# Wide first-layer products for the mixer's spatial tiles and the second gated step, with the halves added on VectorE

## The reference, cut to what matters

```python
def even_mixer(h, w_in, conv_w, pool_w, pool_scale, w_out):
    z = h @ w_in                                  # 256 x 1024 @ 1024 x 2048
    gate_b = z[..., :A_W]                         # A_W = 512
    gate_c = z[..., A_W:2 * A_W]
    val = z[..., 2 * A_W:3 * A_W]
    pool_in = z[..., 3 * A_W:]
    y_a = gate_b * causal_dwconv(gate_c * val, conv_w)
    y_b = multiscale_pool(pool_in, pool_w, pool_scale)
    return jnp.concatenate([y_a, y_b], axis=-1) @ w_out

def conv_ffn(h, w_in, conv_w, conv_b, w_out):     # D_FF = 2816
    z = h @ w_in
    u, g = z[..., :D_FF], z[..., D_FF:]
    a = causal_dwconv(u, conv_w) + conv_b
    return (jax.nn.silu(a) * g) @ w_out
```

## Time and profile before

| | |
|---|---|
| time, median of 3 runs (lowest to highest) | 1242.0 us (1241.77 to 1242.34) |
| span of the profiled execution, first to last instruction | 1240.0 us |
| TensorE matmuls, busy | 1226.5 us, 99% of the span |
| VectorE busy | 967.7 us, 78% |
| ScalarE busy | 703.3 us, 57% |
| GpSimd busy | 135.4 us, 11% |
| DMA | 214 GB/s mean |
| chain that ended last | TensorE 87%, VectorE 8%, ScalarE 2% |

### The profile page before, as it was taken

How to read it: one execution, slowest core, us unless ns; L and a number is a source line. 1 busy time by engine, 2 the same in 40 slices (tenths; PEclk the granted TensorE clock), 3 DMA queues, 4 the chain that set the end, 5 groups by cost and what they waited for, 6 DMA issues and landing times.

```text
span 1240.0 us, 18559 instructions
## 1 busy us (share of the span) xinstructions
PE 1226.5 (99%) x7013; PEld 1063.4 (86%) x7013; DVE 967.7 (78%) x1218; ACT 703.3 (57%) x1061; POOL 135.4 (11%) x249
## 2 busy tenths in 40 slices
PE   8999999999999999999999999999999999999998
PEld 7989888888778989998889888888888998888887
DVE  5867999977885798898788688997685898676654
ACT  6555555556465555555677566555564243755552
POOL 5000000010000211111133201120010010000000
PEclk9999999999999999999999999999999999999999
DMA  9746777665562798893132448997456587386540
GB/s 325 236 153 219 241 248 239 223 198 182 184 204 68 236 331 309 314 334 115 55 122 69 137 170 291 392 391 262 170 200 208 171 309 267 123 292 211 179 160 34
DMA packets 153649, 265.77 MB, mean 214 GB/s; under 512 B 6092, under 2 KB 110480, under 8 KB 153584
## 3 DMA queue, kind: packets, MB, share of 16 engines
q1 hardware_dynamic: 134560, 204.75, 48.8%
q0 software_dynamic: 18544, 59.65, 13.7%
q10 hardware_dynamic: 480, 0.49, 0.1%
HBM read 263.78 MB, written 1.08 MB: 214 GB/s over the span
## 4 chain that ended last, share of the span: by engine, by line
PE 87%; DVE 8%; ACT 2%; issue 2%; POOL 1%; DMA 0%; POOLq 0%; ACTq 0%; DVEq 0%
PE ps L1948 24%; PE ps L1928 17%; PE ps L1931 9%; PE ps L1914 4%; PE ps L1913 4%; PE ps L1912 4%; DVE w_lo L1141 2%; PE ps L1991 2%; PE ps L1992 2%; PE ps L1993 2%; PE ps L2055 2%; PE ps L1969 2%; PE ps L1971 2%; PE ps L1970 2%; PE ps L2057 2%
## 5 line engine op out<-in xcount | busy, mean ns | idle before, releaser
L1141 DVE TENSOR_TENSOR w_lo<-raw,w_hi 128x2048 fp32r<-128x2048 f32 (+3 forms) x211 | 434.1, 2071 | 32.2 <-ACT w_hi L580 31.9
L580 ACT ACTIVATE w_hi<-raw 128x2048 fp32r<-128x2048 f32 (+3 forms) x213 | 368.7, 1737 | 61.6 <-PE ps L1948 51.1
L1928 PE MATMUL ps<-xn,w_hi 128*128 128x512 f32 x976 | 244.9, 393 | 0.1
L1928 PEld LDWEIGHTS ps<-xn,w_hi 128*128 128x128 f32 x976 | 178.3, 189 | 35.3 <-issue 1.6
L1931 PEld LDWEIGHTS ps<-xn,w_lo 128*128 128x128 f32 x976 | 133.1, 190 | 9.6
L1931 PE MATMUL ps<-xn,w_lo 128*128 128x256 f32 x976 | 136.1, 283 | 0.0
L1948 PE MATMUL ps<-w_hi,a_hi 128*128 128x512 f32 x432 | 134.7, 393 | 0.2 <-DVE a_lo L1853 0.2
L661 ACT ACTIVATE work<-ps 128x512 f32<-128x512 f32 x61 | 36.3, 594 | 171.7 <-PE ps L1931 171.7
L1948 PE MATMUL ps<-w_lo,a_hi 128*128 128x512 f32 x432 | 133.6, 390 | 0.0
L1948 PE MATMUL ps<-w_hi,a_lo 128*128 128x512 f32 x432 | 133.3, 390 | 0.0
L1912 PE MATMUL ps<-xn,w_hi 128*128 128x256 f32 x432 | 122.8, 284 | 0.0
(11 more groups left out here) (362 smaller groups left out, 2007.7 us busy)
## 6 DMA issues: line engine op xcount, KB each, us to landing
raw<-in_ffn_w SPq DMA_DIRECT2D x64, 1024.0 KB, 5.6
side<-in_ada_w POOLq DMA_DIRECT2D x96, 512.0 KB, 6.1
raw<-in_ffn_w_in SPq DMA_DIRECT2D x40, 1024.0 KB, 5.2
raw<-in_ffn_w_out SPq DMA_DIRECT2D x32, 512.0 KB, 5.2
raw<-in_gm_w_in SPq DMA_DIRECT2D x16, 1024.0 KB, 6.5
raw<-in_od_w_in SPq DMA_DIRECT2D x12, 1024.0 KB, 5.4
raw<-in_gm_w_out SPq DMA_DIRECT2D x8, 1024.0 KB, 5.7
raw<-in_ev_w_in SPq DMA_DIRECT2D x7, 1024.0 KB, 12.4
```

The costliest lines, as they stand in the source:

```text
L580: nc.scalar.activation(w_hi[s][:, 0:w], raw[s][:, 0:w], ACT.Copy).then_inc(hi_done, 1)
L1141: nc.vector.tensor_tensor(w_lo[s][:, 0:w], raw[s][:, 0:w], w_hi[s][:, 0:w].bitcast(F32), ALU.subtract)\
L1928: nc.tensor.matmul(o, hi, xn[:, 512 * k:512 * k + 512], start=k == 0, stop=False)
```

## The change

1. The six tiles of the first mixer become `f_wide`, into banks 0/1, 4/5, 6/7, 0/1, 2/3, 0/1. ScalarE's copy of gate_c is removed. A new helper `halves_added` adds the two halves of a bank pair in one VectorE instruction, a `tensor_reduce` over a strided view of PSUM: for each output it reads the element at column t and the one at column t + 256. It stands for gate_c (into SBUF), for val and for gate_b (each into `ev_in` in SBUF, followed by the multiplication, which waits for it).
2. TensorE's waits for free banks change with the banks: tile 5 now waits for `EV["gate"]` 1 and tile 7 for `EV["gate"]` 2.
3. Step 1 of the gated layers: the u tile is `f_wide` in both layers, the g tile in the first; `low_copy` and `join` are now also run for step 1, the transposed head goes to banks 4 and 5, and one TensorE wait for `prod` before the loop goes.

The core of the diff:

```diff
-            ev_c = wk(6144, 512)
             ev_cv = wk(2048, 2 * 258).rearrange("p (b t) -> p b t", b=2)
...
             for m in range(2):
                 t = T_EV + 2 + 3 * m
-                act.wait_ge(w_used, t + 1)
-                nc.scalar.activation(ev_c, ps[3 * m % 4][:, :], ACT.Copy).then_inc(EV["gate"], 1)
                 split(t + 4)
...
-                    src = ps[0 if j.c else 2]
-                    if j.c >= 2:
+                    src = ps[4]
+                    if j.c:
                         low_copy(f_u, 0)
...
-                    if j.c >= 2 and n == 0:
+                    if j.c and n == 0:
                         act.wait_ge(w_used, val(u + 2))
                         low_copy(f_g, 2)
...
+            def halves_added(x, bank):
+                v = banks[:, 512 * bank:512 * bank + 1024].rearrange("p (b c t) -> p b t c", b=2, c=2)
+                return nc.vector.tensor_reduce(pair(x), v, AX.X, ALU.add)
...
             for m in range(2):
                 t = T_EV + 2 + 3 * m
+                dve.wait_ge(w_used, t + 1)
+                halves_added(wk(6144, 512), 0).then_inc(EV["gate"], 1)
+                dve.wait_ge(w_used, t + 2)
+                chain(halves_added(ev_in, (4, 2)[m]))
                 dve.wait_ge(EV["gate"], m + 1)
-                dve.wait_ge(w_used, t + 2)
-                nc.vector.tensor_tensor(ev_cv[:, :, 2:258], ps[(1 + 3 * m) % 4][:, :].rearrange("p (b t) -> p b t", b=2),
-                                        ev_c, ALU.mult).then_inc(EV["prod"], 1)
+                nc.vector.tensor_tensor(ev_cv[:, :, 2:258], pair(ev_in), ev_c, ALU.mult).then_inc(EV["prod"], 1)
...
                 dve.wait_ge(w_used, t + 3)
-                nc.vector.tensor_tensor(ev_y, ps[(2 + 3 * m) % 4][:, :], ev_a, ALU.mult).then_inc(EV["y"], 1)
+                chain(halves_added(ev_in, (6, 0)[m]))
+                nc.vector.tensor_tensor(ev_y, ev_in, ev_a, ALU.mult).then_inc(EV["y"], 1)
...
-                    x = ps[0 if j.c else 2]
-                    if j.c >= 2:
+                    x = ps[4]
+                    if j.c:
                         join(f_u, 0, u_join(j))
                         x = f_u
...
-                    x = ps[3 if j.c == 0 else 1 if j.c == 1 else 2]
-                    if j.c >= 2 and n == 0:
+                    x = ps[2 if j.c else 5]
+                    if j.c and n == 0:
                         join(f_g, 2, u_join(j) + 1)
...
-            free = {4: (EV["pool"], 1), 5: (EV["pool"], 2), 6: (EV["gate"], 1), 7: (EV["prod"], 1)}
+            free = {2: (head_cp, 2 * HEAD["ev"] + 1), 5: (EV["gate"], 1), 6: (EV["pool"], 2), 7: (EV["gate"], 2)}
             head("ev", T_EV)
-            for m in range(2, 8):
+            for m, bank in zip(range(2, 8), (0, 4, 6, 0, 2, 0)):
                 if m in free:
                     pe.wait_ge(*free[m])
-                else:
-                    pe.wait_ge(head_cp, 2 * HEAD["ev"] + m - 1)
-                f_tile(T_EV + m, (m - 2) % 4, mid=(lambda: head_out("ev")) if m == 2 else None)
+                f_wide(T_EV + m, bank, mid=(lambda: head_out("ev")) if m == 2 else None)
...
-                        f_tile(u, 0, mid=lambda: head_out(name))
-                        f_tile(u + 1, 1)
+                        f_wide(u, 0, mid=lambda: head_out(name, 4))
+                        f_wide(u + 1, 2) if n == 0 else f_tile(u + 1, 2)
...
                 t_step(Aff(0), 0, first=True)
-                pe.wait_ge(g["prod"], 2)
```

More of the change, by code:

```diff
@@ L312, in build @@
         GM_BANK = [0, 2, 6, 4]
-        J_FFN = [0, 2 * G_STEPS + 2]
-        J_QK = 2 * G_STEPS - 4
-        J_RELU0 = J_FFN[1] + G_STEPS - 2
+        J_FFN = [0, 2 * G_STEPS + 4]
+        J_QK = 2 * G_STEPS - 2
+        J_RELU0 = J_FFN[1] + G_STEPS - 1
         J_RELU1 = J_RELU0 + R_STEPS - 2
@@ L743, in u_join @@
                 def u_join(j):
-                    return j * 2 + (J_FFN[0] - 3) if n == 0 else j + (J_FFN[1] - 1)
+                    return j * 2 + (J_FFN[0] - 1) if n == 0 else j + J_FFN[1]
                 def step(j, par):
@@ L1085, in build @@
         ev_a = wk(6656, 512)
-        ev_y = wk(0, 512)
+        ev_y, ev_in = wk(0, 512), wk(4096, 512)
         ev_u = wk(2564, 4 * 272).rearrange("p (g t) -> p g t", g=4)
@@ L2061, in head, with head_out @@
                         last.then_inc(head_t, 1)
-            def head_out(name):
+            def head_out(name, bank=2):
                 for tt in range(TT):
@@ L2070, in head_out @@
                             c = 512 * tt + 256 * i + P * b
-                            last = nc.tensor.transpose(ps[2 + i][:, b * S + tt * P:b * S + tt * P + P], wk(c, P), ident)
+                            last = nc.tensor.transpose(ps[bank + i][:, b * S + tt * P:b * S + tt * P + P], wk(c, P), ident)
                 last.then_inc(head_ps, 1)
@@ L2108, in later_vec_rows @@
                 last.then_inc(vec_ps, 1)
-            free = {4: (EV["pool"], 1), 5: (EV["pool"], 2), 6: (EV["gate"], 1), 7: (EV["prod"], 1)}
+            free = {2: (head_cp, 2 * HEAD["ev"] + 1), 5: (EV["gate"], 1), 6: (EV["pool"], 2), 7: (EV["gate"], 2)}
             head("ev", T_EV)
-            for m in range(2, 8):
+            for m, bank in zip(range(2, 8), (0, 4, 6, 0, 2, 0)):
                 if m in free:
                     pe.wait_ge(*free[m])
-                else:
-                    pe.wait_ge(head_cp, 2 * HEAD["ev"] + m - 1)
-                f_tile(T_EV + m, (m - 2) % 4, mid=(lambda: head_out("ev")) if m == 2 else None)
+                f_wide(T_EV + m, bank, mid=(lambda: head_out("ev")) if m == 2 else None)
             pe.wait_ge(EV["pool_a"], 1)
-            pe.wait_ge(EV["gate"], 2)
+            pe.wait_ge(EV["prod"], 2)
             pe.wait_ge(EV["y"], 1)
@@ L2133, in _ @@
                 if j == 0:
-                    pe.wait_ge(EV["prod"], 2)
+                    pe.wait_ge(EV["y"], 2)
                     pe.wait_ge(in_small, 16 * 5)
```

## The result

The changed kernel takes 1245.62 us (median of 7 runs, 1244.53 to 1246.32); the kernel before, run beside it, 1241.77 (7 runs). The ratio is 1.003, 95% interval 1.0021 to 1.0039: slower by the prediction's own line of 0.2%, by 3.85 us where 1.7 were forecast. The profiled execution has a span of 1244.6 us against 1240.0.

What follows compares the result with a forecast made beforehand. TensorE's own work was taken to bound the kernel. Stalls of 0.95 and 2.44 us less a saving of 1.67 gave +1.72 on the span of 1240.0: 1242.0 + 1.7 = 1243.7 us, range 1241.5 to 1248.3.

Steps and rivals of the forecast that it cites:

- rival A: VectorE's strided reduction in the mixer costs 2.00 us, with a third stall at tile 10: +5.6, 1247.6 us; chance 0.28.
- The likeliest case: Whole kernel: two mixer stalls less the TensorE saving, +1.72 us, 1243.7 us, within 0.2% of before; chance 0.55.
- the case given 0.04: Anywhere in the kernel: something unforeseen adds more than 1 us; chance 0.04.
- What bounds the kernel: TensorE's own work, busy 1226.5 of 1240.0 us; every stall created in its stream adds to the time.
- The saving: TensorE, nine wide tiles in mixer and gated layers: 0.185 us less each, 1.67 us in all.
- The price of the strided sum: VectorE's six mixer reductions of 1024 read elements to 512 results go by elements read: 1.22 us each.
- B: VectorE's mixer reduction goes by results only, 0.69 us: -0.4, 1241.6 us; chance 0.06 together with rival C.
- rival C: No stall at all in the mixer, only TensorE's saving: -1.67, 1240.3 us; chance 0.06 together with B.
- Stall at tile 5: First mixer: TensorE's tile 5 waits for VectorE's first reduction, queued behind the pooling: 0.95 us.
- Stall at tile 7: First mixer: TensorE's tile 7 reuses banks 0/1 and waits for VectorE's fourth reduction: 2.44 us.
- I give these joins nothing: Step 1 of the gated layers: VectorE's added joins, 0.60 us each, fit in 1.2 us of room; no stall.
- No third stall at tile 10: Mixer: the second group's `a_lo` is ready at 70.63, 0.9 us before TensorE wants tile 10; no wait.

Runs made afterwards that it cites:

- the mixer alone: Changed kernel with the gated layers' tiles, banks and join numbers put back as in the kernel before; 1244.19 us, ratio 1.0023.
- the experiment on the first sum: Changed kernel with VectorE's first strided sum moved ahead of the pooling; 1245.23 us, ratio 1.0029.
- VectorE relieved: Kernel before with both gated layers' second steps wide, three quarters of the second layer's last unit of modulation sums left out; 1241.20 us, ratio 0.9995.
- VectorE burdened: Kernel before plus one useless 0.60 us VectorE sum between the taps in step 8 of the second gated layer; 1242.26 us, ratio 1.0003.
- split sums in other banks: Changed kernel with other bank pairs for mixer tiles 5 to 7, halves copied by ScalarE and added by VectorE at 0.60 us; 1241.56 us, ratio 1.0001.

## Why the prediction was right, and where it was not

**Range and direction** held, the range by luck. 1245.62 lies in 1241.5 to 1248.3, but that range reached so high only to hold rival A, the dear strided sum, and rival A is false. The likeliest case said 1243.7, 1.9 short, and its own range ended at 1244.9. It called for no measurable change (0.54); the outcome, slower by 0.31%, had 0.44. What came true is the forecast's mechanism plus more than 1 us that it didn't foresee, the case given 0.04. In the profiled execution 4.60 us were lost where the sum had 1.72. Of the 2.88 missing, 1.68 are the clock and 0.76 the end of the second gated layer, both terms that the sum put at nothing; 0.41 are the first stall, and 0.03 the rest.

**What bounds the kernel**: right for the mixer. Too coarse for the rest: "no cause makes it wait more than 0.9 us" was read as room, while at the end of the second gated layer TensorE didn't wait only because two times fell together (570.53 and 570.59).

**The saving**: right, 1.62 for 1.67.

**The price of the strided sum**: right, 1.216 us for 1.22. Rivals A and B fall with this row, and rival C with the two waits. What "Vector Engine (DVE) Microarchitecture Reference", section 5.2 "Measured stream behaviour on trn2", of the Trainium skill says of one source that alternates between two far regions, the full rate, is borne out here for two places in PSUM, 256 words apart (the page's lie 16 KiB apart): 1216 ns, against 1220 for 1024 elements in order. Its dear case, 1.73 ns per element where elements in order take 1.05, agrees with L1471's 373 ns for 128 elements against 286 in order, 0.68 ns more per element.

**Stall at tile 5**: right in kind and place, 1.36 for 0.95. It varies with the start of the pooling (a recorded wait of 0.20 with the mixer alone, 1.10 here), which the sum took as fixed at the time of before.

**Stall at tile 7**: right, 2.34 for 2.44. "Tile 7's start no longer depends on the first stall at all" was true of that order of work, but its sequel in the experiment on the first sum, that tile 7 would start no earlier, was wrong: VectorE had idle time ahead of the pooling.

**Clock**: missed. The sum priced a pause by its length alone. In the profiled run TensorE came back from this one at half speed, +1.68 us; by time and mean clock, so it did in six of seven runs. Filling the pause takes the fall away. That it is the pause, and not tile 7 or the DMAs, is shown by this; why it costs the clock in most runs of the change and in few of the mixer alone, is not.

**Gated layers**: the step that failed is "I give these joins nothing", for the second layer. The walk compared the join with what TensorE wants next (the split of step 2), found 1.2 us and stopped there. But "The second layer has the same picture with one join" is wrong in two ways. In the first layer two modulation sums stand between the join and the taps, so that ScalarE's scaling is done in their time, and ahead of the join of step 2 VectorE had 1.69 us of idle time, in which the lateness from step 1 disappears. Before, then in the changed kernel, where TensorE is 4.15 us later and this join too:

```profile
122.72 0.69 DVE L1155 TENSOR_TENSOR work<-ps,work 128x512 f32<-128x512 f32 x1 [1.69 <-ACT work L661]
```

```profile
126.87 0.69 DVE L1152 TENSOR_TENSOR work<-ps,work 128x512 f32<-128x512 f32 x1
```

In the second layer nothing stands between join and taps, and the join costs VectorE 1.16 us more than its own length: ScalarE's scaling, formerly done before VectorE came to the taps, now follows it. And through that layer VectorE has the modulation sums and no idle time except its waits for ScalarE, which follow its own work, and 1.44 us for GpSimd in step 2. So of the 1.92 us that it is late at step 1, about 1.0 goes in the waits for GpSimd, 0.16 in step 8, and 0.76 is handed on to the end of the layer, 150 us later, where TensorE needs its last product at once. The experiments show each link: alone the gated change loses 0.8 us; with only the first layer wide it doesn't; with VectorE relieved it gains 0.5; with VectorE burdened the transposes of the kernel before come 0.33 us late at the same place.

**No third stall at tile 10**: right, and it hung on the two stalls ahead of it: without them it is there (1.8 us).

## What to carry to other kernels

An engine for which nobody waits may be full: look at the last thing it hands over in each stage, here a product that came 0.06 us before its use. A delay put on such an engine is paid where the stage ends and not where it is made. And a new stall on TensorE is priced by its length plus what the clock may lose behind it; here nine filler matmuls (1244.33 us) were cheaper than the pause that they filled (1245.62), and split sums in other banks cheaper than either (1241.56).

## What the runs showed of the hardware

- A pause of TensorE of 2.17 us was followed by 3.5 us at a granted clock of 0.52 (1.2 GHz), 1.68 us lost; pauses of 2.15 and 2.36 us in two other profiles were not. In the runs time and mean clock tell of a fall in 6 of 7 executions of the change, and in none of 11 with nine matmuls in the pause. What decides it, no run here shows.
- VectorE's sum of two halves in PSUM, 256 words apart, 1024 elements read to 512, takes 1216 ns, as 1024 elements in order (1220): this stride costs nothing. L1471, four places 32 words apart in on-chip memory and 128 elements, takes 373 ns, where 128 in order take 286.
- Some executions of kernels without a long pause are 1.2 to 1.7 us slower at a clock of 1.0 (three of eleven with the fillers). Left open.
